# The inverses of an RWKV-7 chunk recurrence kept in 32 columns through four levels, with products over all four matrices' columns laid at steps of 96

## The chip, the cores and the metric

One core of one Trainium2 chip. The metric is the device time of one execution in microseconds. The kernel computes three layers (an RWKV-7 time mix, a differential attention, a gated linear recurrence with a spatial gate), each with its feed-forward part, on 256 tokens of width 1024, all in fp32.

## The reference, cut to what matters

The change lies in the RWKV-7 time mix: sixteen heads of 64 channels, 256 tokens, one token after another:

```
def step(state, inp):
    r_t, w_t, k_t, v_t, a_t, b_t = inp
    sa = jnp.einsum('bhvk,bhk->bhv', state, a_t)
    state = (state * w_t[:, :, None, :]
             + sa[..., None] * b_t[:, :, None, :]
             + v_t[..., None] * k_t[:, :, None, :])
    y_t = jnp.einsum('bhvk,bhk->bhv', state, r_t)
    return state, y_t
```

The kernel does it in chunks of 128 tokens. Within a chunk, `sa` of a token depends on `sa` of all earlier tokens through a strictly triangular 128x128 matrix A (products of `a` of one token and `b` of another, with the decay between them), so it needs the inverse of I - A, one for each head and chunk.

## The kernel before, in words

**Engines and order.** Each engine has its own program, written out by hand, and runs it strictly in order. Engines meet by semaphores. The eight PSUM banks are handed out ahead of time: `place(key, banks)` lists the jobs of each bank in their order; TensorE waits until the last use of the bank is freed (`open_bank`) and signals when its products are in (`close`); the reader waits for that (`wait_full`) and frees the bank (`release`). There are no costs or due times: what stands next on an engine is next.

**The recurrence.** It works on four pairs of groups (`PAIRS`, p = 0 to 3). A group `g` is 128 channels, so two heads; with two chunks of 128 tokens it has four matrices A, numbered j. For each pair:

1. Scores (L865 to L868): four products for each matrix, of 64 rows, into one bank. VectorE multiplies the bank with a mask of triangles (L2022) and so puts `scores` in SBUF. TensorE then does a stage of another kind, `project_r(p + 1)`, the projection for the next pair (three products at a time, L638 to L640); in pair 3 it does `y_centre` (L817) instead, whose results ScalarE writes in seven pieces of work (`y_square`, L1370 and L1371, and a table load).
2. The inverse of I - A, by doubling. `x` holds the inverse of the diagonal blocks of 2^l tokens, `xt` its transpose. A level l joins two neighbouring blocks: `y` is the product of A, as it lies in `scores`, with `xt` (L889), copied by ScalarE to SBUF (L1410), then `dx` = `y` with `x` (L901), of which VectorE takes the blocks of this level with a predicated copy (`joined`, L2029) and transposes 32x32 blocks (`turned`, L2025) to have `xt` for the next level. Up to block size 32 that transpose is all within 32x32 blocks (levels 0 to 4, below `SQUARE = 5`). At level 5 the blocks are 64 wide, so TensorE transposes (L912) and ScalarE copies (L1415). At level 6 only the corner of 64x64 is wanted: `y` (L891), the copy, `dxt` (L903), and VectorE's copy L2053.
3. The states and outputs: `q0`, `sa0`, `st`, `q1`, `sa1`, `yt` (L941 to L965), each one after another, with ScalarE's copies (L1441) and VectorE's L2079.

`x`, `xt` and `y` of one group are each 128x512: four matrices of 128 columns side by side, in `work[:, g % 2, i, :]`. Outside the diagonal blocks they are zero. Each level does group 0 of the pair, then group 1: eight `y` products, then eight `dx` products (four each).

**Side work.** Between the levels of pair p stands what prepares pair p + 1: on VectorE `decay_scan` (L1920) after level 1, `key_floor` (L1937) and `decay_centre` after 2, `decay_ends` after 3, `keys_unit` after 4, `keys_scaled` and `bonus_terms` after 5, the four `tilde` products after 6; on ScalarE the split of a weight unit (L1211) after 1, `key_log` (L1340) after 2, which waits for `key_floor`, `key_root` (L1344) after 3, `decay_now` after 4, `decay_sums` (L1358, L1360) after 5; on TensorE `key_sum` (L782) after 1.

Of the kernel before, what the change touches and what calls it, by code (L numbers as in the profile page):

```python
# [8 lines left out]
I32 = mybir.dt.int32  # L9
# [13 lines left out]
SQUARE = 5  # L23
NG = KT
# [48 lines left out]
CONS = [("ident", P), ("ones", P), ("head_sum", P), ("right_left", LEV * P), ("left_right", LEV * P), ("score_mask", 4 * P), ("centre", P), ("rope_swap", P), ("cos", S), ("sin", S)]  # L73
# [76 lines left out]
def build(nc, wide, down, x_t, ctx_t, cols, cons, rows, w_sp, out):  # L150
    with ExitStack() as ctx:
# [125 lines left out]
        for p, pair in enumerate(PAIRS):  # L277
# [12 lines left out]
            for l in range(1, LEV):  # L290
                for what in ("y", "dx") if l < SQUARE else ("y", "dx", "xt") if l < LEV - 1 else ("y", "dxt"):
                    for g in pair:
                        place((what, g, l), CHAIN_BANKS)
# [203 lines left out]
        y_sq = buf[1]  # L497

# [84 lines left out]
        with nc.Block() as block:  # L583
# [31 lines left out]
            def _(pe):  # L615
# [238 lines left out]
                for p, pair in enumerate(PAIRS):  # L854
                    nxt = p + 1 < len(PAIRS)
                    pe.wait_ge(sem("tilde_ready"), 4 * p + 4)
                    for g in pair:
                        for c in range(2):
                            for hd in range(2):
# [5 lines left out]
                                mm(bank[:, 0:P], at_, bt_, start=True, stop=True)  # L865
# [12 lines left out]
                    for l in range(1, LEV):  # L878
                        for g in pair:
                            xt = work[:, g % 2, 2, :]  # L880
                            if l <= SQUARE:
                                pe.wait_ge(sem(f"xt_ready{g % 2}"), SQUARE * (g // 2) + l)
                            else:
                                wait_freed(pe, ("xt", g, l - 1))
                            bank = open_bank(("y", g, l))
                            for j in range(4):
                                s_ = slice(j * P, (j + 1) * P)
                                if l < LEV - 1:
                                    last = mm(bank[:, s_], scores[g % 2][:, j, 0:P], xt[:, s_], start=True, stop=True)  # L889
# [3 lines left out]
                        for g in pair:  # L893
                            _, x, xt, y = (work[:, g % 2, i, :] for i in range(4))
                            wait_freed(pe, ("y", g, l))
                            what = "dx" if l < LEV - 1 else "dxt"
                            bank = open_bank((what, g, l))
                            for j in range(4):
                                s_ = slice(j * P, (j + 1) * P)
                                if what == "dx":  # L900
                                    last = mm(bank[:, s_], y[:, s_], x[:, s_], start=True, stop=True)  # L901
                                else:
                                    last = mm(bank[0:CH, j * CH:(j + 1) * CH], x[0:CH, j * P:j * P + CH], y[0:CH, j * CH:(j + 1) * CH], start=True, stop=True)  # L903
                            close(last, (what, g, l))
                        if SQUARE <= l < LEV - 1:
                            for g in pair:
                                x = work[:, g % 2, 1, :]
                                wait_freed(pe, ("dx", g, l))
                                bank = open_bank(("xt", g, l))
                                for j in range(4):  # L910
                                    s_ = slice(j * P, (j + 1) * P)
                                    last = nc.tensor.transpose(bank[:, s_], x[:, s_], ident)  # L912
                                close(last, ("xt", g, l))
# [148 lines left out]
                def context_states(c):  # L1062
                    if c == 4:
                        pe.wait_ge(sem("ctx_log"), 1)
                        for d in range(2):
                            tri = const("score_mask", (0, 2)[d] * P)
# [118 lines left out]
            def _(eng):  # L1185
# [160 lines left out]
                def units(g):  # L1346

                    act_(work[:, g % 2, 1, :].rearrange("p (j n) -> p j n", j=4), spread(ident, [P, 4, P]), ACT.Copy).then_inc(sem("unit_x"), 1)
# [42 lines left out]
                for p, pair in enumerate(PAIRS):  # L1391
# [13 lines left out]
                    for l in range(1, LEV):  # L1405
                        for g in pair:
                            key = ("y", g, l)
                            wait_full(eng, key)
                            m, n = (P, 512) if l < LEV - 1 else (CH, 4 * CH)
                            release(act_(work[0:m, g % 2, 3, 0:n], bank_of(key)[0:m, 0:n], ACT.Copy), key)  # L1410
                        if SQUARE <= l < LEV - 1:
                            for g in pair:
                                key = ("xt", g, l)
                                wait_full(eng, key)
                                release(act_(work[:, g % 2, 2, :], bank_of(key)[:, :], ACT.Copy), key)  # L1415
# [1155 lines left out]
```

## Time and profile before

| | us |
|---|---|
| median of 3 runs | 1399.5 (1395.93 to 1400.88) |
| the profiled execution's own time | 1391.34 |
| its span | 1389.3 |
| recurrence within the span, from the first scores (L865) to the last `yt` (L965) | about 99.5 to 324 |

Busy over the span: TensorE 1253.1 us (90%), VectorE 937.6 (67%), ScalarE 634.1 (46%), GpSimd 206.5 (15%). The chain of work that ended last is 64% TensorE, 24% VectorE, 7% ScalarE. An fp32 product has two records on TensorE. Records of one line that follow each other are merged, so `x8` beside L889 is four products; the time of such a row holds the tail of its last product. The granted clock is given as a share of full speed (2.4 GHz); 0.50 is 1.2 GHz.

### The profile page before, as it was taken

The page shows a single profiled execution, that of the slowest core. Times are in us where ns is not written, and L with a number is a line of the kernel's source. Part 1 is how long each engine was busy: PE and PEld are TensorE (multiplying, and loading weights), DVE is VectorE, ACT ScalarE, POOL GpSimd, SP SyncE. Part 2 cuts the span into 40 slices and gives each one's busy share as a digit, 9 for nine tenths or more (in the row PEclk, how much of TensorE's full clock was granted, in tenths as well). Part 3 has the DMA queues.
Part 4 walks back from the last instruction along what each step waited for, and adds up shares of the span by engine and source line. Part 5 has one row for each costly group of instructions (what it writes and reads, how often), then busy time and mean ns, then how long its engine had stood idle before and what let it go on. Part 6 is the DMA issues. An engine that isn't in the chain of part 4 may idle for free.

```text
span 1389.3 us, 21888 instructions
## 1 busy us (share of the span) xinstructions
PE 1253.1 (90%) x9218; PEld 1165.7 (84%) x9218; DVE 937.6 (67%) x1294; ACT 634.1 (46%) x835; POOL 206.5 (15%) x139
## 2 busy tenths in 40 slices
PE   4998988989899999699878889999789887999995
PEld 3887878777899999696658888999789877999995
DVE  6767566554478874646864666874558835999994
ACT  4464343253543445555555565434433234544442
POOL 0000000000454441000000111210000002344431
PEclk9999999899899999899998999999899998999998
DMA  7441001001676654253223677875333213555530
GB/s 270 146 162 33 32 1 62 1 1 48 244 250 247 243 183 152 93 186 115 98 89 119 212 267 269 292 276 183 109 138 113 74 57 121 183 170 184 185 130 31
DMA packets 122656, 200.26 MB, mean 144 GB/s; under 512 B 3264, under 2 KB 111168, under 8 KB 112320
## 3 DMA queue, kind: packets, MB, share of 16 engines
q1 hardware_dynamic: 117664, 168.11, 35.8%
q0 software_dynamic: 3456, 25.17, 4.8%
q10 hardware_dynamic: 1440, 5.60, 1.1%
q8 instruction: 73, 1.20, 0.3%
q14 instruction: 23, 0.19, 0.0%
HBM read 197.82 MB, written 1.05 MB: 143 GB/s over the span
## 4 chain that ended last, share of the span: by engine, by line
PE 64%; DVE 24%; ACT 7%; issue 4%; DMA 0%; DVEq 0%; POOL 0%; ACTq 0%
PE bank L638 13%; PE bank L639 12%; PE bank L640 12%; DVE buf L2453 7%; DVE ring_r L1760 6%; PE bank L721 3%; PE bank L723 3%; PE bank L722 3%; ACT high L1211 3%; PE bank L901 2%; DVE work L2029 2%; PE bank L654 2%; DVE work L2025 2%; PE bank L889 2%; PE bank L1103 1%
## 5 line engine op out<-in xcount | busy, mean ns | idle before, releaser
L638 PE MATMUL bank<-part,high 128*128 128x256 f32 x1664 | 486.8, 293 | 58.9 <-DVE part L1767 51.1
L1760 DVE TENSOR_TENSOR ring_r<-ring,high 128x2048 fp32r<-128x2048 f32 (+1 forms) x155 | 343.8, 2227 | 205.8 <-ACT high L1211 203.5
L639 PE MATMUL bank<-part,high 128*128 128x256 f32 x1664 | 481.7, 290 | 0.0
L640 PE MATMUL bank<-part,ring_r 128*128 128x256 f32 x1664 | 481.2, 289 | 0.0
L638 PEld LDWEIGHTS bank<-part,high 128*128 128x128 f32 x1664 | 330.9, 199 | 66.0 <-issue 41.9
L639 PEld LDWEIGHTS bank<-part,high 128*128 128x128 f32 x1664 | 331.0, 199 | 1.3 <-issue 1.2
L640 PEld LDWEIGHTS bank<-part,ring_r 128*128 128x128 f32 x1664 | 330.7, 199 | 0.0
L1211 ACT ACTIVATE high<-ring 128x2048 fp32r<-128x2048 f32 x155 | 295.1, 1906 | 51.1 <-PE bank L640 40.9
L1687 POOL TENSOR_TENSOR ring_r<-ring,high 128x512 fp32r<-128x512 f32 x44 | 92.7, 2107 | 523.4 <-ACT high L1211 523.3
L721 PE MATMUL bank<-part,high 128*128 128x256 f32 x528 | 151.3, 286 | 9.2 <-POOL part L1681 4.9
L722 PE MATMUL bank<-part,high 128*128 128x256 f32 x528 | 150.1, 284 | 0.0
L723 PE MATMUL bank<-part,ring_r 128*128 128x256 f32 x528 | 150.0, 284 | 0.0
L1681 POOL TENSOR_TENSOR part<-buf,part 128x256 fp32r<-128x256 f32 x66 | 100.0, 1517 | 224.6 <-ACT part L1266 224.6
L721 PEld LDWEIGHTS bank<-part,high 128*128 128x128 f32 x528 | 102.1, 193 | 10.2 <-POOL part L1681 5.2
L2453 DVE SCALAR_TENSOR_TENSOR buf<-buf,col 128x256 f32<-128x256 f32 x176 | 106.6, 606 | 5.5
L722 PEld LDWEIGHTS bank<-part,high 128*128 128x128 f32 x528 | 102.1, 193 | 0.3 <-issue 0.2
L723 PEld LDWEIGHTS bank<-part,ring_r 128*128 128x128 f32 x528 | 102.0, 193 | 0.0
L2109 DVE SCALAR_TENSOR_TENSOR buf<-buf,buf 128x1024 f32<-128x1024 f32 x64 | 100.2, 1565 | 1.4
L1266 ACT ACTIVATE part<-buf 128x256 fp32r<-128x256 f32 x66 | 27.5, 417 | 150.5 <-DVE buf L1821 150.5
L638 PE MATMUL bank<-high,part 128*128 128x512 f32 x144 | 60.1, 418 | 0.4 <-DVE buf L2172 0.4
L639 PE MATMUL bank<-ring_r,part 128*128 128x512 f32 x144 | 57.8, 401 | 0.0
L640 PE MATMUL bank<-high,part 128*128 128x512 f32 x144 | 57.6, 400 | 0.0
(267 smaller groups left out, 1568.5 us busy)
## 6 DMA issues: line engine op xcount, KB each, us to landing
ring<-in_wide SPq DMA_DIRECT2D x122, 1024.0 KB, 5.9
ring<-in_down SPq DMA_DIRECT2D x33, 1024.0 KB, 4.9
buf<-in_wide POOLq DMA_DIRECT2D x24, 1024.0 KB, 7.2
con<-in_cons SPq DMA_DIRECT2D x1, 1536.0 KB, 11.1
ring<-in_wide SPq DMA_DIRECT2D x2, 576.0 KB, 7.0
buf<-in_wide ACTq DMA_DIRECT2D x1, 1024.0 KB, 5.1
buf<-in_wide SPq DMA_DIRECT2D x1, 1024.0 KB, 5.2
buf<-in_ctx_t ACTq DMA_DIRECT2D x1, 1024.0 KB, 7.3
```

The lines of the kernel that those rows point to most:

```text
L638: mm(bank, ah, bh, start=start, stop=False, skip_group_check=shared)
L639: mm(bank, ah, bl, start=False, stop=False, skip_group_check=shared)
L640: return mm(bank, al, bh, start=False, stop=stop, skip_group_check=shared)
L721: mm(bank, wh, act_high(f), start=f == 0 and cb % 2 == 0, stop=False, skip_group_check=True)
L722: mm(bank, wh, act_low(f), start=False, stop=False, skip_group_check=True)
L723: return mm(bank, wl, act_high(f), start=False, stop=f == FT - 1, skip_group_check=True)
L1211: act_(hi, raw, ACT.Copy).then_inc(sem("unit_high"), 1)
L1681: nc.gpsimd.tensor_tensor(act_low(f), act_value(f), act_high(f).bitcast(F32), ALU.subtract).then_inc(sem("act_ready"), 1)
L1687: nc.gpsimd.tensor_tensor(low, raw, hi.bitcast(F32), ALU.subtract).then_inc(sem("unit_low_rest"), 1)
L1760: v.tensor_tensor(low, raw, hi.bitcast(F32), ALU.subtract).then_inc(sem("unit_low"), 1)
L2109: own.step(v.scalar_tensor_tensor(flat(buf[6])[:, 0:D], w, 1.0, silu_row[:, which, :], ALU.mult, ALU.mult, accum_out=ada[:, 4 * c + 2 * ha ...
L2453: ins = v.scalar_tensor_tensor(acc, view, pcol("conv_w", 9 * f + n), acc, ALU.mult, ALU.add)
```

## The change

- `x` is kept in 32 columns a matrix through levels 0 to 4 (`work[:, g % 2, 3, P:2P]`, 128 columns for the four matrices): row i holds the 32 columns of its own diagonal block of 32. `y` is kept likewise. `xt` stays at full width (512 columns).
- A product takes the 128x128 matrix of one j as the stationary side and the 128 columns of all four matrices as the moving side. Of the result only the 32 columns of matrix j are wanted; it is laid at column 96 j, so that these land at column 128 j, and the next product overwrites what isn't wanted.
- The stationary side of `y` is now A masked to its 32x32 diagonal blocks (`near`), and at level 5 A's blocks beside them (`far`), which ScalarE copies during level 1 (`far_blocks`).
- Level 0 goes into `xt` first and is transposed back to `x`. At levels 1 to 4 the join writes `x` (128 columns), and four transposes of 32 partitions each write `xt`. The product `y` waits for `x` alone, the product `dx` for `xt`.
- Level 5 has no transpose on TensorE: `corner` products and `dx` products give the two orientations. ScalarE copies `x`'s diagonal and the corner into `left_of(g)`, VectorE transposes two blocks a group into `xt`.
- The scores' matrix A is formed the other way round, and one more 64x64 product a matrix gives the corner in the first orientation. The constants grow by `later`, `near` and `joins`; four memsets are added at the start; the context sums read `later`.

The diff, cut to its core:

```
 for l in range(1, LEV):
-    for what in ("y", "dx") if l < SQUARE else ("y", "dx", "xt") if l < LEV - 1 else ("y", "dxt"):
+    for what in ("y", "dx") if l < SQUARE else ("y", "corner", "dx") if l < LEV - 1 else ("y", "dxt"):
...
 y_sq = buf[1]
+def chain_parts(g):
+    t = work[:, g % 2]
+    return t[:, 0, :], t[:, 1, :], t[:, 2, :], t[:, 3, 0:P], t[:, 3, P:2 * P]
+def left_of(g):
+    return work[0:CH, g % 2, 3, 2 * P:4 * P].rearrange("p (j n) -> p j n", j=4)
+def wide_y(g):
+    return work[0:CH, g % 2, 3, 0:4 * CH]
+def own_cols(j):
+    return slice(j * (P - SQ), j * (P - SQ) + P)
+def own_squares(t):
+    return t.rearrange("p (j n) -> p j n", j=4)[:, :, 0:SQ]
+def squares(t):
+    return t.rearrange("p (j n) -> p j n", j=4)
...
 at_, bt_, kt_, rt_ = (z[part, g, tok] for z in (kk_t, b_t, k_t, r_t))
-mm(bank[:, 0:P], at_, bt_, start=True, stop=True)
+mm(bank[:, 0:P], bt_, at_, start=True, stop=True)
+mm(bank[CH:P, 0:CH], at_[:, CH:P], bt_[:, 0:CH], start=True, stop=True)
...
 for g in pair:
-    xt = work[:, g % 2, 2, :]
+    near, far, xt, _, x = chain_parts(g)
     if l <= SQUARE:
-        pe.wait_ge(sem(f"xt_ready{g % 2}"), SQUARE * (g // 2) + l)
+        pe.wait_ge(sem(f"x_ready{g % 2}"), SQUARE * (g // 2) + l)
     else:
-        wait_freed(pe, ("xt", g, l - 1))
+        wait_freed(pe, ("dx", g, SQUARE))
+    if l == SQUARE:
+        pe.wait_ge(sem(f"far_ready{g % 2}"), g // 2 + 1)
         if l < LEV - 1:
-            last = mm(bank[:, s_], scores[g % 2][:, j, 0:P], xt[:, s_], start=True, stop=True)
+            last = mm(bank[:, own_cols(j)], (near if l < SQUARE else far)[:, s_], x, start=True, stop=True)
 for g in pair:
-    _, x, xt, y = (work[:, g % 2, i, :] for i in range(4))
+    _, _, xt, y, _ = chain_parts(g)
     wait_freed(pe, ("y", g, l))
+    if l <= SQUARE:
+        pe.wait_ge(sem(f"xt_ready{g % 2}"), SQUARE * (g // 2) + l)
+    else:
+        wait_freed(pe, ("corner", g, SQUARE))
+    if l == SQUARE:
+        bank = open_bank(("corner", g, l))
+        for j in range(4):
+            last = mm(bank[0:CH, own_cols(j)], xt[:, j * P:j * P + CH], y, start=True, stop=True)
+        close(last, ("corner", g, l))
     for j in range(4):
-        s_ = slice(j * P, (j + 1) * P)
-        if what == "dx":
-            last = mm(bank[:, s_], y[:, s_], x[:, s_], start=True, stop=True)
+        if l < SQUARE:
+            last = mm(bank[:, own_cols(j)], xt[:, j * P:(j + 1) * P], y, start=True, stop=True)
+        elif what == "dx":
+            last = mm(bank[0:P - SQ, own_cols(j)], xt[:, j * P + SQ:(j + 1) * P], y, start=True, stop=True)
         else:
-            last = mm(bank[0:CH, j * CH:(j + 1) * CH], x[0:CH, j * P:j * P + CH], y[0:CH, j * CH:(j + 1) * CH], start=True, stop=True)
+            last = mm(bank[0:CH, j * CH:(j + 1) * CH], left_of(g)[:, j, :], wide_y(g)[:, j * CH:(j + 1) * CH], start=True, stop=True)
     close(last, (what, g, l))
-if SQUARE <= l < LEV - 1:
-    for g in pair:
-        x = work[:, g % 2, 1, :]
-        wait_freed(pe, ("dx", g, l))
-        bank = open_bank(("xt", g, l))
-        for j in range(4):
-            s_ = slice(j * P, (j + 1) * P)
-            last = nc.tensor.transpose(bank[:, s_], x[:, s_], ident)
-        close(last, ("xt", g, l))
...
 def units(g):
-    act_(work[:, g % 2, 1, :].rearrange("p (j n) -> p j n", j=4), spread(ident, [P, 4, P]), ACT.Copy).then_inc(sem("unit_x"), 1)
+    act_(squares(chain_parts(g)[2]), spread(ident, [P, 4, P]), ACT.Copy).then_inc(sem("unit_x"), 1)
+def far_blocks(g):
+    eng.wait_ge(sem("scores_in"), g + 1)
+    far = squares(chain_parts(g)[1])
+    own.go(act_(far[0:SQ, :, SQ:CH], scores[g % 2][0:SQ, :, SQ:CH], ACT.Copy))
+    act_(far[CH:CH + SQ, :, CH + SQ:P], scores[g % 2][CH:CH + SQ, :, CH + SQ:P], ACT.Copy).then_inc(sem(f"far_ready{g % 2}"), 1)
+def left_diagonal(g):
+    eng.wait_ge(sem(f"x_ready{g % 2}"), SQUARE * (g // 2) + SQUARE)
+    x = squares(chain_parts(g)[4])
+    for b in range(2):
+        r = slice(b * SQ, (b + 1) * SQ)
+        own.go(act_(left_of(g)[r, :, r], x[r, :, :], ACT.Copy))
+def left_corner(g):
+    key = ("corner", g, SQUARE)
+    wait_full(eng, key)
+    release(act_(left_of(g)[SQ:CH, :, 0:SQ], own_squares(bank_of(key)[SQ:CH, :]), ACT.Copy), key)
...
     wait_full(eng, key)
-    m, n = (P, 512) if l < LEV - 1 else (CH, 4 * CH)
-    release(act_(work[0:m, g % 2, 3, 0:n], bank_of(key)[0:m, 0:n], ACT.Copy), key)
-if SQUARE <= l < LEV - 1:
+    if l < LEV - 1:
+        release(act_(squares(chain_parts(g)[3]), own_squares(bank_of(key)[:, :]), ACT.Copy), key)
+    else:
+        release(act_(wide_y(g), bank_of(key)[0:CH, 0:4 * CH], ACT.Copy), key)
+if l == 1:
     for g in pair:
-        key = ("xt", g, l)
-        wait_full(eng, key)
-        release(act_(work[:, g % 2, 2, :], bank_of(key)[:, :], ACT.Copy), key)
+        far_blocks(g)
+if l == SQUARE:
+    for g in pair:
+        left_diagonal(g)
+    own.settle()
+    for g in pair:
+        left_corner(g)
...
     own.go(v.memset(ap, value))
+for i in range(2):
+    own.go(v.memset(work[:, i, 1, :], 0.0))
+    own.go(v.memset(work[0:CH, i, 3, 2 * P:4 * P], 0.0))
...
         release(v.tensor_tensor(scores[g % 2][:, j, :], bank_of(key)[:, :], const("score_mask", 0, 512), ALU.mult), key)
-def turned(g):
-    v.transpose(work[:, g % 2, 2, :], work[:, g % 2, 1, :]).then_inc(sem(f"xt_ready{g % 2}"), 1)
-def joined(g, l, block):
-    return v.copy_predicated(work[:, g % 2, 1, :].rearrange("p (j n) -> p j n", j=4),
-                             spread(const("right_left", l * P), [P, 4, P]).bitcast(I32), block)
+def turned(g, back):
+    xt, x = squares(chain_parts(g)[2]), squares(chain_parts(g)[4])
+    for b in range(4):
+        r = slice(b * SQ, (b + 1) * SQ)
+        dst, src = (xt[r, :, r], x[r, :, :])[::-1 if back else 1]
+        ins = v.transpose(dst, src)
+        own.go(ins) if b < 3 else ins.then_inc(sem(f"{'x' if back else 'xt'}_ready{g % 2}"), 1)
 for g in pair:
+    near, _, xt, _, _ = chain_parts(g)
         wait_freed(eng, ("sc", g, j))
-    own.step(joined(g, 0, scores[g % 2][:, :, 0:P]))
-    turned(g)
+    eng.sem_inc(sem("scores_in"), 1)
+    v.copy_predicated(squares(xt), spread(const("left_right"), [P, 4, P]).bitcast(I32), scores[g % 2][:, :, 0:P])\
+        .then_inc(sem(f"xt_ready{g % 2}"), 1)
+    own.go(v.tensor_tensor(squares(near), scores[g % 2][:, :, 0:P], spread(const("near"), [P, 4, P]), ALU.mult))
+    eng.wait_ge(sem(f"xt_ready{g % 2}"), SQUARE * (g // 2) + 1)
+    own.settle()
+    turned(g, True)
     for g in pair:
-        if l < LEV - 1:
+        if l < SQUARE:
             wait_full(eng, key)
-            release(joined(g, l, bank_of(key)[:, :].rearrange("p (j n) -> p j n", j=4)), key)
-            if l < SQUARE:
-                wait_freed(eng, key)
-                turned(g)
+            x = squares(chain_parts(g)[4])
+            block = own_squares(bank_of(key)[:, :])
+            v.copy_predicated(x, spread(const("joins", (l - 1) * SQ, SQ), [P, 4, SQ]).bitcast(I32), block).then_inc(sem(f"x_ready{g % 2}"), 1)
+            eng.wait_ge(sem(f"x_ready{g % 2}"), SQUARE * (g // 2) + l + 1)
+            eng.sem_inc(free[jobs[key][0]], 1)
+            turned(g, False)
+        elif l == SQUARE:
+            key = ("dx", g, l)
+            wait_full(eng, key)
+            xt = squares(chain_parts(g)[2])
+            block = own_squares(bank_of(key)[:, :])
+            own.go(v.transpose(xt[0:SQ, :, SQ:CH], block[0:SQ]))
+            release(v.transpose(xt[CH:CH + SQ, :, CH + SQ:P], block[CH:CH + SQ]), key)
             wait_full(eng, key)
-            wait_freed(eng, ("xt", g, l - 1))
+            wait_freed(eng, ("dx", g, SQUARE))
...
 z["left_right"] = np.concatenate([m.T for m in lv], 1)
-z["score_mask"] = np.concatenate([i > j, i <= j, i < j, i <= j], 1)
+z["score_mask"] = np.concatenate([(i < j) | ((i >= CH) & (j < CH)), i <= j, i < j, i <= j], 1)
+z["later"] = i > j
+z["near"] = (i < j) & (i // SQ == j // SQ)
+z["joins"] = np.concatenate([np.take_along_axis(m, i // SQ * SQ + np.arange(SQ)[None, :], 1) for m in lv[1:SQUARE]], 1)
```

## Rows read from the trace of the kernel before

**Rows 1.** Chain of waits, pair 2, level 4: start, duration (us), engine, tile, line.
```profile
238.47 1.16 PE bank L889 x8
239.62 0.91 PE bank L901 x8
...
240.56 0.75 DVE work L2029
...
241.33 0.71 DVE work L2025
242.04 0.63 DVE work L2029
...
242.69 0.72 DVE work L2025
```

**Rows 2.** Chain of waits, pair 2, from level 2 to level 3.
```profile
232.59 0.59 DVE buf L1937
...
233.20 0.63 ACT buf L1340
...
234.37 1.17 PE bank L901 x8
```

**Rows 3.** Chain of waits, pair 2, levels 5 and 6.
```profile
243.46 1.16 PE bank L889 x8
244.61 1.86 PE bank L901 x16
...
248.57 0.53 ACT buf L1358
...
249.12 0.63 ACT buf L1360
...
250.07 1.14 PE bank L903 x16
```

**Rows 4.** Windows, levels of pairs 2 and 3: columns as the view's heading.
```profile
core 0: us, PE busy (x) PEld busy (x) DVE busy (x) ACT busy (x) POOL busy (x), PEclk, DMA share, GB/s
221.70:251.20 29.50, 25.05 (x205) 21.96 (x203) 19.69 (x35) 15.88 (x25) 0.00 (x0) 1.00 0.21 72
278.90:309.80 30.90, 26.59 (x208) 22.82 (x207) 14.18 (x21) 15.32 (x26) 0.00 (x0) 1.00 0.00 1
```

**Rows 5.** Groups by shape, 98 to 344 us: busy, mean ns; idle before.
```profile
L2029 DVE COPY_PREDICATED work<-con,bank 128x512 f32<-128x512 int32 x40 | 28.7, 718 | 40.4 <-PE bank L901 40.3
L2025 DVE STREAM_TRANSPOSE work<-work 128x512 f32<-128x512 f32 x40 | 28.5, 712 | 1.4
...
L1441 ACT ACTIVATE work<-bank 128x128 f32<-128x128 f32 x32 | 8.9, 278 | 23.3 <-PE bank L944 12.6 <-PE bank L951 10.6
...
L2079 DVE SCALAR_TENSOR_TENSOR work<-bank,tiny,con 128x128 f32<-128x128 f32 x8 | 2.8, 351 | 11.8 <-PE bank L955 11.8
```

**Rows 6.** Timeline of VectorE, pair 2: start, time of all, line, shape, count.
```profile
212.07 4.87 DVE L2022 TENSOR_TENSOR buf<-bank,con 128x512 f32<-128x512 f32 x8 [5.19 <-PE bank L868]
...
227.53 1.33 DVE L1920 TENSOR_TENSOR_SCAN buf<-con,buf 128x128 f32<-128x128 f32 x4
```

**Rows 7.** Timeline of ScalarE, pair 3, first copies of level 1.
```profile
281.77 1.08 ACT L1410 ACTIVATE work<-bank 128x512 f32<-128x512 f32 x2
```

**Rows 8.** Timeline of TensorE, in pair 2 and in pair 3.
```profile
225.44 1.02 PE L782 MATMUL bank<-buf,con 128*128 128x512 f32 x2
...
286.88 1.95 PE L889 MATMUL bank<-work,buf 128*128 128x128 f32 x16
```

**Rows 9.** Windows around and after the levels; PEclk is the granted clock.
```profile
196.00:208.00 12.00, 12.00 (x79) 10.62 (x77) 6.57 (x10) 3.86 (x11) 0.00 (x0) 0.72 0.01 1
248.00:252.00 4.00, 3.15 (x39) 2.80 (x39) 2.62 (x6) 2.42 (x6) 0.00 (x0) 0.98 0.01 4
250.00:266.00 16.00, 15.93 (x71) 10.90 (x72) 6.14 (x9) 2.55 (x9) 0.00 (x0) 0.68 0.00 1
308.00:324.00 16.00, 15.53 (x124) 12.11 (x124) 11.02 (x23) 5.50 (x16) 0.00 (x0) 1.00 0.00 1
```

More of the change, by code:

```diff
@@ L23 @@
 SQUARE = 5
+SQ = 32
 NG = KT
@@ L71 @@
         ("conv_b", FT), ("conv_w", 9 * FT), ("b_ada", 48)]
-CONS = [("ident", P), ("ones", P), ("head_sum", P), ("right_left", LEV * P), ("left_right", LEV * P), ("score_mask", 4 * P), ("centre", P), ("rope_swap", P), ("cos", S), ("sin", S)]
+CONS = [("ident", P), ("ones", P), ("head_sum", P), ("right_left", LEV * P), ("left_right", LEV * P), ("score_mask", 4 * P), ("centre", P), ("later", P), ("near", P), ("joins", (SQUARE - 1) * SQ), ("rope_swap", P), ("cos", S), ("sin", S)]
 ROWS = [("sgu_g", 512), ("sgu_b", 512), ("b_spatial", 512), ("lam", 256), ("c", 2 * D)]
@@ L1065, in context_states @@
                         for d in range(2):
-                            tri = const("score_mask", (0, 2)[d] * P)
+                            tri = const(("later", "score_mask")[d], (0, 2)[d] * P)
                             for t in range(TT):
```

## The prediction, as it was made

> **What bounds the kernel now.** I read the page first: TensorE is on 64% of the chain that ended last and VectorE on 24% (the table above). The change touches only the recurrence, so I then read the chain of waits there. In one middle level of a pair's inverses [rows 1] it is a closed loop: the second group's product L889, the first group's product L901, then four VectorE instructions in a row (join L2029 and transpose L2025, for the first group and the second). 243.46 (rows 3) - 238.47 = 5.0 us per level, of which VectorE has 2.8 us; TensorE's sixteen products need only 3.6 us (below). Level 3 is longer [rows 2]: key_floor L1937 stands on VectorE behind both groups, ScalarE's logarithm L1340 waits for it, and the copy of `y` (L1410) stands behind L1340; L901 waits for that copy. Levels 5 and 6 [rows 3] add transposes on TensorE (L912) with their copy L1415, and ScalarE's two exponentials L1358 and L1360 stand ahead of the level-6 copy, for which L903 waits. From the first product to the end of the last level it is 29.5 us for pair 2 (pairs 0 and 1 are alike within 0.1 us) and 30.9 us for pair 3 [rows 4]; TensorE is busy 85% of it, tails of waiting products included, so there is air of at least 4.4 us a pair.
>
> **Prices.** Back-to-back, sixteen records of 128-column products (two records a product, eight products) take 1.86 us with the tail [rows 3], so four products cost 0.9 us and a level's sixteen 3.6 us. Eight 64x64 products take 1.14 us [rows 3], with little tail 1.0. VectorE: a 128x512 join or transpose takes 718 or 712 ns, a 128x128 operation out of PSUM 351 ns [rows 5]. Back-to-back the cost is lower than the duration: eight 128x512 instructions in 4.87 us are 0.6 us each, four 128x128 scans in 1.33 us are 0.31 us each but for the tail [rows 6]. ScalarE: two copies of 128x512 take 1.08 us [rows 7], one of 128x128 278 ns [rows 5].
>
> **TensorE's work hardly changes.** The products of levels 1 to 4 keep 128 moving columns, four per group: same count, same price. Level 5 gets eight corner products (1.8 us) for eight transposes on TensorE, which are no dearer; the sum below counts the new ones in full. Scores get one 64x64 product for each of eight matrices of a pair: between 0.5 us (the two row halves overlap) and 1.0 us (1.14 us per eight, rows 3); I take 0.8 us. For pairs 0 to 2 it is on the path, because TensorE runs from scores through project_r without a gap into L889 at 221.70, where the stretch of rows 4 begins. For pair 3 it delays y_centre and so the seven ScalarE pieces that end at 281.77 [rows 7]: also 0.8 us.
>
> **VectorE, levels 1 to 4.** The join shrinks from 128x512 to 128x128: 0.35 us. The one transpose becomes four of 32x128 elements. The trace has no such row. Cheapest it is 0.2 us each (128 of the 512 elements of the 0.6 us rate, plus that rate's rest of 0.07 us), dearest 0.63 us (no cheaper than the whole one at its own rate, 712 ns less the 0.08 us overlap). I take 0.21 to 0.23, nearest to the scans and the 0.6 us row: 0.85 us for four, 1.2 us per group instead of 1.45. The larger gain is order: L889 now needs only the join (`x`), and the transposes `xt` are wanted only by the product after it, 1.8 us later. So per level, counted from the end of a group's second product: join to 0.35; TensorE is still in the other group's product until 0.9; transposes to 1.2; second group's join 1.2 to 1.55, wanted at 1.8. Nothing waits, ScalarE's copies (0.28) included: a level costs TensorE's 3.6 us.
> The Trainium skill, "VectorE: DVE Perf Modes", section on the TRN2 errata, says a fixed latency is paid per instruction, so many small tiles pay it each time, and gives about 150 cycles as the measured fixed part. By that (an estimate from the page) a transpose is 0.29 us, four are 1.16, and each level with side work on VectorE loses about another 0.5 us: some 4 us of the gain would go. The trace's 0.6 us rate [rows 6] says that back-to-back most of that term overlaps; the scans at 0.31 us stand nearer to the page.
>
> **The sum for a pair with a successor (0 to 2).** Level 1: 3.6 plus key_sum's one product of 512 columns, 1.02 us [rows 8] less its tail of some 0.16, so 4.45. Level 2: 3.6. Level 3: 3.6 plus the stall of rows 2, which stays: after the second product of level 2, VectorE has 2.4 us of joins and transposes and 0.65 us key_floor, ScalarE 0.65 us logarithm and 0.3 us copy, 4.0 us, where TensorE would want `y` at 2.7; so +1.35 (counted from the first group's product; until then TensorE has three groups' products of 0.9). Level 4: 3.6. Level 5: twenty-four products, 5.4. Level 6: two times 1.0 us, 0.2 us in which the second group's last two transposes are late, 0.3 us for the copy, 2.5 us. The exponentials L1358 and L1360 (1.16 us in the chain [rows 3]) start after left_corner, beside the second group's last products, and are done when the level-6 products are: they leave the path, and cost up to 1.2 us a pair if ScalarE is later than that. Loose ends 0.2. Total 24.7 against 29.5: 4.8, less 0.8 for scores, 4.0 us; three pairs 12.0 us.
> Pair 3 has no key_floor. Its levels 2 to 6 run from 286.88 [rows 8] to 309.8, 22.9 us; new 3 x 3.6 + 5.4 + 2.5 + 0.1 = 18.8. That saves 4.1, less 0.8: 3.3 us.
> Other edits cost nothing in their cover. The start of a pair: join L2029, the mask `near` and four transposes make 2.2 us per group instead of 1.4, so `x` of the second group is ready 4.4 us after the eighth score mask; VectorE finishes the masks at 216.9 [rows 6], so 221.4, ahead of 222.5 when L889 can start (221.70 plus 0.8). Uncovered it would be 1.6 us a pair; in pair 3, ScalarE's busy time to 281.77 covers it. far_blocks (four ScalarE copies, about 0.8 us per pair) fits in level 1; left_diagonal and left_corner lie beside the level-5 products. VectorE's keys_scaled and bonus_terms (five instructions, about 2.3 us) now end up to 1.3 us after L2053 is wanted; sa0 waits for L2053, but q0's products, about 1 us, come first, so 0.3 us, taken from the loose ends. Four memsets at the very start (under 2 us by the 0.6 us rate) lie beside the load of the input; uncovered they cost that once. The masks' load grows by 384 columns (196 KB on 1536) and is first needed far later.
> Together 15.3 us.
>
> **The clock.** After the level chains of pairs 0, 1 and 2 the granted clock falls to 0.50, the 1.2 GHz level, so that it is 0.72 over 12 us after pair 1 (pair 0 the same) and 0.68 over 16 us after pair 2, yet stays at 1.00 after pair 3 [rows 9]. In the 4 us before the third fall TensorE was busy 3.15 us. A mean of 0.72 over 12 us is 6.7 us at the low level, so at most 3.4 us lost; 0.68 over 16 us is 10.2, at most 5.1: together 11.9 us at stake. What pair 3 lacks before this place is just the wait behind L1358 and L1360, and that wait goes. The new levels also leave TensorE fewer pauses. But level 6 stays thin. The gain lies between 0 and 11.9 us; I take 5, a little under half, since parts of these stretches hang on ScalarE and VectorE.
> The Trainium skill, "TensorE: Matmul & The Clock Gate", on HAM oscillation, ties the fall to idle gaps between bursts; row 248:252 shows a fall with no such gap, so it gives no reason for the falls to go. By the page alone the clock term would be nothing.
>
> **Sum.** 15.3 + 5 = 20.3 us. The profiled execution took 1391.3 us (span 1389.3), so 1371.0. The median of three runs is 1399.5, 8 us above it; the saving carries over: 1379 us. What follows the recurrence starts earlier as a whole, as its first weights wait in the ring (SyncE's queue issues next to nothing in this stretch).
>
> **Rivals.**
> A. The clock stays full after all three pairs, and the waits shrink as counted: 15.3 + 11.9 = 27, 1372. For: pair 3. Against: thin level 6. Chance 0.18.
> B. Clock unchanged and VectorE as dear as the scans, so that levels 1 to 4 with side work are VectorE-bound: the scan rate makes 8 x 0.1 = 0.8 us more a level, of which side work exposes some 2 us a pair: 15.3 - 7 = 8 us, 1391. Chance 0.13.
> C. Slower: a small transpose costs as much as the whole one, 0.63 us. Then VectorE has 2 x (0.35 + 2.5) = 5.7 us per level plus side work (0.6 to 1.4 us in each of levels 1 to 4, as key_floor in rows 2 and the scans in rows 6), 27 us for four levels where it was 21.8 (221.70 to 243.46): with the scores +6 a pair, 1423 us. It decides from about 0.45 us per transpose on. Against: every other VectorE row shrinks with its elements [rows 5, 6]. Chance 0.05.
> D. The change doesn't shorten anything: as the products stay 128 columns wide, TensorE's busy time stays, and were TensorE the bound, only the added products would show: +3 us, 1402. Against: 15% air and rows 1. Chance 0.03.
> The forecast, 1379 (own range 1373 to 1387), has 0.61.
>
> Range 1367 to 1393: it takes in A and B, leaves C and D out. Under 0.3% (4.2 us) I could not tell from no change. Faster 0.92, same 0.03, slower 0.05.
>
> **What would show it.** Right: the level loop at 3.6 us with L889 following a join, not a transpose; a 32-partition transpose at 0.2 to 0.3 us; ScalarE's `y` copy at 0.28 us; a remaining TensorE wait of about 1.3 us before the second product of level 3; the stretches of rows 4 at 24 to 25 us; project_r 0.8 us later after the scores. Wrong: transposes of 0.4 us or more, chain steps at the transposes, scores that lose the overlap of their two row halves (over 1.5 us a pair), or new falls of the clock elsewhere.

## The result, and the profile after

The changed kernel takes 1411.8 us (median of 4 runs, 1410.9 to 1416.9) where the kernel before, beside it, takes 1400.2 (4 runs, 1395.9 to 1401.2): ratio 1.0097, 95% interval 1.0065 to 1.0128. It is slower by 11.6 us; forecast was 1379, faster by 20, in a range of 1367 to 1393. The sign is wrong.

The page of the profiled execution (1416.9 us, the highest of the four; the profiled execution of before was at 1391.3 among the lowest, so the two profiles differ by 25.8 us of span where the medians differ by 11.6; the mean granted clock of this execution is 0.942, of the other three 0.948 to 0.949):
```profile
PE 1282.1 (91%) x9314; PEld 1190.2 (84%) x9314; DVE 955.2 (67%) x1434; ACT 629.3 (44%) x867; POOL 206.4 (15%) x139
PE 65%; DVE 23%; ACT 6%; issue 5%; DMA 0%; DVEq 0%; POOL 0%; ACTq 0%
```

Windows of the profile after: the scores of pairs 0 to 3, then the levels of pairs 0 to 3 (start:end and length, then each engine's busy time and count, the granted clock, the DMA share and GB/s).
```profile
99.39:108.81 9.42, 9.42 (x82) 7.79 (x81) 6.49 (x8) 3.43 (x4) 0.00 (x0) 1.00 0.34 113
...
220.69:235.42 14.73, 14.73 (x81) 12.08 (x81) 4.84 (x7) 0.00 (x0) 0.00 (x0) 0.58 0.00 1
293.15:302.56 9.41, 9.41 (x82) 7.79 (x81) 4.84 (x7) 0.60 (x1) 0.00 (x0) 1.00 0.01 2
...
116.33:146.98 30.65, 27.29 (x213) 24.85 (x211) 20.59 (x60) 14.78 (x33) 0.00 (x0) 0.89 0.11 36
176.10:207.32 31.22, 27.62 (x213) 25.15 (x211) 20.94 (x63) 14.78 (x33) 0.00 (x0) 0.89 0.11 35
243.28:272.73 29.45, 26.20 (x213) 23.87 (x211) 20.00 (x59) 14.76 (x33) 0.00 (x0) 0.94 0.21 73
305.97:336.84 30.87, 27.82 (x215) 24.52 (x215) 16.26 (x51) 13.21 (x32) 0.00 (x0) 0.94 0.00 1
```
The levels were to shrink from 29.5 (pair 3: 30.9) [rows 4] to 24.7 (26.8) and have not shrunk: 122.2 us for the four pairs where before they took 119.4. By their granted clocks (each window times one minus its clock) at most 10.4 of the 122.2 us are the low clock's; before, the levels ran at full clock. The scores take 9.4 us a pair at full clock where before they took 5.0 (99.48 to 104.5 in the trace of before, for pair 0), and 14.7 us in pair 2, mostly at the low clock. With project_r behind pair 2's scores, 2.1 us slower for the same clock, the profiles' account is 22.9 (scores) + 2.1 + 2.8 (levels) = 27.8 us; the recurrence ends 27.0 us later (last L994 product at 350.74, before at 323.7). Everything is in the recurrence.

Two places explain it. **First the scores.** TensorE's timeline, one key (the products of one matrix) from 99.39 on:
```profile
99.39 0.48 PE L890 MATMUL bank<-buf,buf 64*128 64x128 f32 x2
99.81 0.33 PE L891 MATMUL bank<-buf,buf 64*64 64x64 f32 x2
100.06 0.49 PE L892 MATMUL bank<-buf,buf 64*128 64x128 f32 x2
...
100.61 0.38 PE L894 MATMUL bank<-buf,buf 64*128 64x128 f32 x2
100.92 0.33 PE L891 MATMUL bank<-buf,buf 64*64 64x64 f32 x2
```
From L891 to the next L891 it is 1.11 us. The same stretch of before:
```profile
100.25 0.27 PE L868 MATMUL bank<-buf,buf 64*128 64x128 f32 x1
100.36 0.27 PE L866 MATMUL bank<-buf,buf 64*128 64x128 f32 x1
100.37 0.27 PE L868 MATMUL bank<-buf,buf 64*128 64x128 f32 x1
100.47 0.27 PE L866 MATMUL bank<-buf,buf 64*128 64x128 f32 x1
```
There two products run at once, one in each 64-row half (records of L866 and L868 start 0.01 to 0.11 us apart), and a key, four products, comes every 0.55 us. After, L890 to L892 stand alone one behind the other; only the end of a key overlaps with the start of the next.

**Then VectorE in the levels.** Its timeline after, pair 1, levels 1 and 2:
```profile
179.19 0.30 DVE L2110 COPY_PREDICATED work<-con,bank 128x128 f32<-128x128 int32 x1 [2.08 <-PE bank L937]
179.64 1.31 DVE L2086 STREAM_TRANSPOSE work<-work 32x128 f32<-32x128 f32 x4
180.98 0.30 DVE L2110 COPY_PREDICATED work<-con,bank 128x128 f32<-128x128 int32 x1
181.43 1.30 DVE L2086 STREAM_TRANSPOSE work<-work 32x128 f32<-32x128 f32 x4
182.77 1.37 DVE L1976 TENSOR_TENSOR_SCAN buf<-con,buf 128x128 f32<-128x128 f32 x4
...
184.25 0.29 DVE L2110 COPY_PREDICATED work<-con,bank 128x128 f32<-128x128 int32 x1
```
A group is 1.79 us (179.19 to 180.98): join 0.30, 0.15 to the first transpose, then four transposes that start 0.33 us apart. Two groups are 3.58, as much as TensorE's whole level, and the scans with their copy (1.5 us) come on top: 5.06 us from level to level, no less than before [rows 1]. The groups by shape say the same; the y copy came out as costed:
```profile
L2086 DVE STREAM_TRANSPOSE work<-work 32x128 f32<-32x128 f32 x160 | 48.4, 303 | 10.0 <-DVE work L2110 1.0
...
L1457 ACT ACTIVATE work<-bank 128x128 f32<-128x128 f32 x40 | 10.7, 274 | 36.1 <-PE bank L917 35.7
```
The chain of waits after, pair 1, from level 2 to level 4 (start, duration, what):
```profile
186.03 0.31 DVE work L2110
186.39 0.44 issue
186.82 0.30 DVE work L2086
...
187.82 0.31 DVE work L2086
188.16 0.70 DVE buf L1993
188.89 0.63 ACT buf L1369
189.52 0.17 ACT work L1457
189.73 3.78 PE bank L937 x16
193.52 2.90 PE bank L917 x16
196.42 0.91 PE bank L937 x8
```
This is the place of [rows 2]: key_floor (L1993) behind the transposes, logarithm, y copy. TensorE's timeline shows what it costs there, in idle time and behind it:
```profile
189.73 3.78 PE L937 MATMUL bank<-work 128*128 128x128 f32 x16 [2.19 <-ACT work L1457]
193.31 3.11 PE L917 MATMUL bank<-work 128*128 128x128 f32 x16
196.25 1.95 PE L937 MATMUL bank<-work 128*128 128x128 f32 x16
```
Sixteen records are 1.95 us at full clock and 3.78 behind the 2.19 us wait. The windows give the granted clock:
```profile
186.00:190.00 4.00, 1.43 (x9) 1.24 (x10) 2.89 (x7) 1.10 (x4) 0.00 (x0) 0.86 0.03 6
190.00:194.00 4.00, 4.00 (x20) 4.00 (x21) 1.81 (x6) 1.78 (x2) 0.00 (x0) 0.50 0.00 0
...
222.00:238.00 16.00, 16.00 (x85) 13.54 (x82) 7.24 (x12) 0.00 (x0) 0.00 (x0) 0.53 0.00 1
```
After a 2.19 us pause the clock is at 0.50, the 1.2 GHz level; and it is at 0.53 over 16 us of pair 2's scores and project_r, in which TensorE never paused.

### The profile page after: what moved, and what is told of

Its sections match the earlier page's. It is cut to its first block, busy times and chain, and to the rows that moved or that the text cites. A ratio compares the mean times of both kernels' runs of the same rounds, so it can differ in the third digit from the quotient of the medians.

```text
span 1415.1 us, 22296 instructions
## 1 busy us (share of the span) xinstructions
PE 1282.1 (91%) x9314; PEld 1190.2 (84%) x9314; DVE 955.2 (67%) x1434; ACT 629.3 (44%) x867; POOL 206.4 (15%) x139
## 4 chain that ended last, share of the span: by engine, by line
PE 65%; DVE 23%; ACT 6%; issue 5%; DMA 0%; DVEq 0%; POOL 0%; ACTq 0%
PE bank L663 12%; PE bank L664 12%; PE bank L665 12%; DVE buf L2525 7%; DVE ring_r L1813 6%; PE bank L746 3%; PE bank L748 3%; PE bank L747 3%; ACT high L1240 3%; DVE work L2086 2%; PE bank L917 2%; PE bank L679 2%; PE bank L937 2%; PE bank L1132 1%; PE bank L892 1%
## 5 line engine op out<-in xcount | busy, mean ns | idle before, releaser
L1295 ACT ACTIVATE part<-buf 128x256 fp32r<-128x256 f32 x66 | 27.5, 417 | 150.6 <-DVE buf L1874 150.6
## 6 DMA issues: line engine op xcount, KB each, us to landing
con<-in_cons SPq DMA_DIRECT2D x1, 1728.0 KB, 11.6
```

## The experiments

Theory T: two terms were mis-sized. The odd-shaped score product ends the overlap of the two row halves (some 17 us), and the small transposes make VectorE the bound of the levels. Rivals: only one of them counts, or the clock alone. Each ratio is to the kernel before, run on the same chip beside it.

**1. The extra score product taken out of the change.** Level 6 is turned so that it needs no corner of the scores.
```diff
-mm(bank[CH:P, 0:CH], at_[:, CH:P], bt_[:, 0:CH], start=True, stop=True)
...
-last = mm(bank[0:CH, j * CH:(j + 1) * CH], scores[g % 2][CH:P, j, 0:CH], xt[CH:P, j * P + CH:(j + 1) * P], start=True, stop=True)
+last = mm(bank[CH:P, j * CH:(j + 1) * CH], scores[g % 2][0:CH, j, CH:P], left_of(g)[:, j, :], start=True, stop=True)
...
-last = mm(bank[0:CH, j * CH:(j + 1) * CH], left_of(g)[:, j, :], wide_y(g)[:, j * CH:(j + 1) * CH], start=True, stop=True)
+last = mm(bank[0:CH, j * CH:(j + 1) * CH], wide_y(g)[:, j * CH:(j + 1) * CH], xt[CH:P, j * P + CH:(j + 1) * P], start=True, stop=True)
```


> The changed kernel without the extra 64x64 score product: level 6 takes its block of A in the new orientation, with the inverse's left half (left_of) as the moving side, so the full result is still computed. Theory T (the extra product breaks the overlap of the two heads' row halves in the scores: 9.4 us a pair instead of 5.0): scores back to 5.0 us, 17 us less than the changed kernel, about 1394. Rival R (the score product costs only its columns, 0.8 us a pair, and the slowdown comes from the clock's falls and from the levels): 3 us less than the changed kernel, about 1408, and slower than before.

Measured: 1390.9 us (12 runs), ratio 0.9952 [0.9931, 0.9973]; against the changed kernel's 1.0097 that is 1.45%, 20 us. The scores are back at 5.0 us in every pair, the levels stay at 28.7 to 32.9. The score product alone costs more than the whole loss. Pair 0's levels rose to 32.9: with short scores the start of a pair is uncovered (below).

**2. The product put into the kernel before.**
```diff
+mm(bank[CH:P, 0:CH], at_[:, CH:P], bt_[:, 0:CH], start=True, stop=True)
 mm(bank[:, 0:P], at_, bt_, start=True, stop=True)
```


> The kernel before with one unused 64x64 score product a matrix put ahead of the first one, whose result is overwritten. T: scores at 9.4 us a pair, 17 us slower than before, about 1417. R: 0.5 to 1.0 us a pair, 1402 to 1404.

Measured: 1439.3 us (5 runs), ratio 1.0311 [1.0282, 1.0339]: +42 us, over twice what T gave. In the timeline of TensorE no two keys' products run at once any more, 1.34 us a key, so 10.7 us a pair at full clock:
```profile
169.25 0.33 PE L865 MATMUL bank<-buf,buf 64*64 64x64 f32 x2
169.50 0.48 PE L866 MATMUL bank<-buf,buf 64*128 64x128 f32 x2
...
170.27 0.38 PE L869 MATMUL bank<-buf,buf 64*128 64x128 f32 x2
170.59 0.33 PE L865 MATMUL bank<-buf,buf 64*64 64x64 f32 x2
```
The rest is the clock: in each pair's scores it falls, with TensorE busy throughout.
```profile
...
169.25:183.56 14.31, 14.31 (x82) 12.24 (x81) 4.84 (x7) 0.60 (x1) 0.00 (x0) 0.72 0.00 1
234.44:251.60 17.16, 17.16 (x81) 14.66 (x81) 4.84 (x7) 0.00 (x0) 0.00 (x0) 0.57 0.00 1
...
```
The scores of pairs 0 and 3 take 14.9 and 13.4 us (granted clock 0.69 and 0.78). Together the four are 59.7 us where before they were 20, so 39.7 of the 42 us. Place inside a key matters too: as the first product the odd one costs 5.7 us a pair, as the second (after) 4.4.

**3. The same product in the upper half of the output.**
```diff
+mm(bank[0:CH, 0:CH], at_[:, 0:CH], bt_[:, 0:CH], start=True, stop=True)
 mm(bank[:, 0:P], at_, bt_, start=True, stop=True)
```


> The kernel before with an unused 64x64 score product a matrix ahead of the first, as e2_before_corner, but laid in the upper half of the partitions. If the smaller shape of the product ends the overlap: 10.7 us of scores a pair, as e2. If it was its place in the lower half alone: about 6 us a pair, as e6.

Measured: 1438.3 us in one run, scores 13.4 to 17.8 us a pair, as in 2. Where the output lies is not it.

**4. The extra product with 128 stationary columns, as its neighbours.**
```diff
+mm(bank[:, 0:CH], at_, bt_[:, 0:CH], start=True, stop=True)
 mm(bank[:, 0:P], at_, bt_, start=True, stop=True)
```


> The kernel before with an unused extra score product a matrix as in e2_before_corner, at the same place, but with a stationary side of 64x128 as the other score products have (64 moving columns), where e2 had 64x64 laid in the lower half of the partitions. If it is the change of the tile's shape that ends the overlap of the two heads' products: overlap stays, scores 5.5 to 6.5 us a pair, 1399 to 1403. If any fifth product does it: 10 to 11 us a pair as in e2, 1435 or more.

Measured: 1397.9 us (10 runs), ratio 1.0004 [0.9983, 1.0025]; scores 6.8 us a pair:
```profile
99.33:106.14 6.81, 6.81 (x82) 6.69 (x81) 4.28 (x5) 3.43 (x4) 0.00 (x0) 1.00 0.48 157
```
More arithmetic, and 1.8 us a pair instead of 5.7: the cost is the change of the stationary operand's shape between 64x128 and 64x64, not the product.

**5. The corner products of two matrices together at the end**, so that the shape changes once per two keys.
```diff
-    mm(bank[CH:P, 0:CH], at_[:, CH:P], bt_[:, 0:CH], start=True, stop=True)
...
-    close(mm(bank[:, 3 * P:4 * P], kt_, rt_, start=True, stop=True), key)
+    mm(bank[:, 3 * P:4 * P], kt_, rt_, start=True, stop=True)
+for hd in range(2):
+    key = ("sc", g, 2 * c + hd)
+    part = slice(hd * CH, hd * CH + CH)
+    at_, bt_ = (z[part, g, c * P:(c + 1) * P] for z in (kk_t, b_t))
+    close(mm(bank_of(key)[CH:P, 0:CH], at_[:, CH:P], bt_[:, 0:CH], start=True, stop=True), key)
```


> The changed kernel with the two heads' 64x64 score products of a chunk put after the eight others of that chunk. T: the eight others overlap as before (1.2 us a chunk, 5.0 a pair), the two extra ones cost at most 0.25 us each: scores about 6 to 7 us a pair, 1400 to 1403. If the order has nothing to do with it (each change of tile shape costs the same wherever it stands): 9.4 us a pair, 1412 as the changed kernel.

Measured: 1404.9 us (7 runs), ratio 1.0047 [1.0015, 1.0079], 0.5% better than the change, though the intervals overlap; scores 7.7 us a pair, 1.8 us of the extra 4.4 gone. With half the changes of shape less is paid. But the two corner products that now stand together also run at once (four records of L898 in 0.33 us), so this run does not part the number of changes from the time of the odd products themselves.

**6. One transpose per join instead of four, score product kept.** The inverses of blocks 0 to 2 are left out.
```diff
-for b in range(4):
+for b in range(4) if back else (3,):
```


> The changed kernel with one of the four 32-partition transposes a join (blocks 0 to 2 are left out, so the inverses are wrong). If levels 1 to 4 are bound by VectorE (0.30 + 0.15 + 4 x 0.334 = 1.8 us a group, 3.6 us a level and side work on top), three transposes less take 2.0 us off VectorE's level: levels 1 to 4 shrink by 1 to 2 us each where there is side work, 12 to 20 us in all, about 1395. If they are bound by TensorE (3.6 us) and the stall at level 3, under 5 us, 1407 or more.

Measured: 1401.4 us (12 runs, 1385.8 to 1407.2; 1398.9 without the two at 1407, which the ratio leaves out too), ratio 1.0001 [0.9970, 1.0032], 13 us better than the change by the ratios. Pair 0's levels:
```profile
116.33:140.98 24.65, 23.76 (x213) 22.04 (x211) 13.33 (x36) 14.68 (x33) 0.00 (x0) 1.00 0.14 44
```
The other pairs: 24.9, 24.65 and 27.5. That is the predicted 24.7, so with cheap transposes the sum is reached in all; its terms are not all met, as the wait of TensorE before the second product of level 3 is 0.61 us here and not 1.35. By these windows 20.5 us left the levels of the four pairs, yet the two spans differ by 15.8. The scores of pair 2 stay at 14.9 us at the low clock, and behind pair 3's levels stands a fall that the change's execution does not have:
```profile
314.00:330.00 16.00, 16.00 (x49) 10.68 (x49) 7.36 (x16) 2.12 (x7) 0.00 (x0) 0.50 0.00 0
```

**7. The transposes made in another way** (in the change as it is): one 128x128 transpose straight from the product's bank, then one masked copy that lays the four blocks.
```diff
-eng.wait_ge(sem(f"x_ready{g % 2}"), SQUARE * (g // 2) + l + 1)
+own.step(v.transpose(turned_block(g), bank_of(key)[:, :].rearrange("p (j n) -> p j n", j=4)[:, :, 0:SQ]))
...
-turned(g, False)
+v.copy_predicated(wide(chain_parts(g)[2]), const("left_right", l * P)..., turned_block(g)...).then_inc(sem(f"xt_ready{g % 2}"), 1)
```


> The changed kernel, its extra score product kept, with the four small transposes of levels 1 to 4 replaced as in e7_one_turn. If the two faults are separate, it gains on the changed kernel what e7 gained on e4, 13 us: about 1399, levels of 26 us, scores still 9.4 us a pair. If the long scores already give VectorE its time back or the clock falls elsewhere, it gains less than 7 us, 1405 or more.

Measured: 1400.3 us (8 runs), ratio 1.0024 [1.0005, 1.0043], 10 us better than the change; levels 26.05 in pairs 0 to 2 and 27.9 in pair 3, at full clock. The ratio's interval lies wholly under the change's [1.0065, 1.0128].

**8. Both mended** (1 and 7).

> e4_level6_turned with the four 32-partition transposes of levels 1 to 4 replaced by one transpose of 128x128 out of PSUM into a spare tile (0.30 us) and one predicated copy of 128x512 from it into xt (0.6 to 0.7 us). Theory T (VectorE's 1.8 us a group, of which the four transposes are 4 x 0.334, sets the levels): a group costs 1.3 to 1.4 us, levels fall from about 30 us a pair to 26 to 28, 6 to 12 us less than e4, 1380 to 1385. Rival (the stall before the second product of level 3 and the fall of the clock behind it hold the levels, whatever the transposes cost): within 3 us of e4.

Measured: 1377.6 us (6 runs), ratio 0.9870 [0.9840, 0.9901]; levels 27.4, 26.0, 26.0 and 29.0. By ratios the score product is worth 1.45%, the transposes 0.73%, both together 2.27%: the two faults add, neither hides the other. The wait of TensorE before the second product of level 3 is 1.34 us in pairs 0 to 2, as predicted (1.35).

**9. key_floor one level earlier** (in 1), so that its logarithm no longer stands ahead of level 3's y copy.
```diff
 if l == 1:
     decay_scan(p + 1)
-elif l == 2:
     key_floor(p + 1)
+elif l == 2:
     decay_centre(p + 1)
```


> e4_level6_turned with key_floor taken from behind level 2 to behind level 1 on VectorE, so that ScalarE's logarithm no longer waits for the joins and transposes of level 2. If the 2.2 us in which TensorE waits at level 3 are that wait, and the clock falls because of it: no wait over 1 us there, no fall of the clock inside the levels of pairs 0 to 2, 2 us and up to 3 us of clock a pair, 1376 to 1384 in all. If VectorE's queue as a whole is the bound, the wait only moves to level 2 and the gain is under 3 us.

Measured: 1382.1 us (6 runs), ratio 0.9901 [0.9868, 0.9934], 7 us better than 1 by the ratios, with intervals that just overlap. Levels 30.6, 27.1, 27.1 and 29.1, in pairs 1 to 3 at a granted clock of 1.00 where 1 had 0.89, 1.00 and 0.94 (pair 0: 0.94, in 1 0.90). In pair 1 the fall went with the stall. That the stall brings it is likely, not shown: in pair 2 of run 1 the clock stays at 1.00 behind such a wait,
```profile
238.19 2.05 PE L936 MATMUL bank<-work 128*128 128x128 f32 x16 [1.84 <-ACT work L1456]
```
and pair 3, which has no key_floor, has a wait of 1.6 us in the change and in 1, 6, 7, 8, 9 and 11, with a fall behind it in the change, in 1 and in 8 and none in the other four. The transposes are as dear as they were.

**10. The same move in the kernel before.**

> The kernel before with key_floor taken from behind level 2 to behind level 1, as in e8_floor_early. If the gain of that move belongs to the new levels only (in the old ones the wait at level 3 is 0.56 us of TensorE): 1 us a pair, 3 us in all, 1394. If it is worth there what it brought on e4: 9 us less than before, 1388.

Measured: 1395.7 us (12 runs), ratio 1.0003 [0.9983, 1.0022]: levels 0.4 to 0.8 us shorter in pairs 0 to 2, nothing that shows in the time; the 3 us that were expected lie just outside the interval (at most 2.4 us). In this execution the granted clock is 0.50 over 306 to 326 us, behind pair 3's levels, where the kernel before has 1.00 in its trace.

**11. Everything mended:** 8 and 9, and ScalarE's key_square behind the first y copies instead of ahead of them.
```diff
 if nxt:
     side_out("r", p + 1, piece(r_t, p + 1))
-    key_square(p + 1)
...
 if l == 1:
+    if nxt:
+        key_square(p + 1)
     for g in pair:
         far_blocks(g)
```


> Both of the last two, and ScalarE's key_square behind the two y copies of level 1 instead of ahead of them. If their gains add: 1370 to 1378, with levels of pairs 0 to 2 at about 25 us, as the prediction had them. If one takes the place of the other: within 3 us of the better one.

Measured: 1374.6 us (6 runs), ratio 0.9832 [0.9797, 0.9868]: the fastest of all, 1.7% under the kernel before. Windows of its levels (the profiled execution is the fastest of the six, 1366.8 us):
```profile
112.56:138.38 25.82, 24.56 (x213) 22.37 (x211) 19.50 (x50) 15.02 (x33) 0.00 (x0) 1.00 0.13 42
160.58:184.71 24.13, 24.03 (x213) 22.23 (x211) 17.88 (x46) 15.02 (x33) 0.00 (x0) 1.00 0.13 45
...
257.99:285.59 27.60, 25.99 (x215) 23.16 (x215) 13.74 (x35) 13.01 (x31) 0.00 (x0) 1.00 0.00 1
```
In pairs 1 and 2 TensorE is busy 24.0 of 24.1 us: now it is the bound, at full clock. VectorE's group in its timeline:
```profile
168.11 0.29 DVE L2114 COPY_PREDICATED work<-con,bank 128x128 f32<-128x128 int32 x1
168.31 0.31 DVE L2115 STREAM_TRANSPOSE turn_tmp<-bank 128x128 f32<-128x128 f32 x1
168.76 0.75 DVE L2118 COPY_PREDICATED work<-con,turn_tmp 128x512 f32<-128x512 int32 x1
169.41 0.28 DVE L2114 COPY_PREDICATED work<-con,bank 128x128 f32<-128x128 int32 x1
```
1.30 us from group to group instead of 1.79. A 128x128 transpose takes 0.31 us, as long as a 32x128 one, and here it starts 0.20 us after the 0.29 us join: these two overlap, where the four small ones (each on 32 other partitions) do not. What keeps those apart no run tests.

## Why the prediction was wrong

**"Scores get one 64x64 product ... I take 0.8 us": the step that turned the sign.** I priced the product by its own rows [rows 3] and never asked what it does to its neighbours. It costs 4.4 us a pair at full clock (17.6 in all where 3.2 stood), because the products around it no longer run two at a time; 1, 2 and 4 show it from three sides, and 5 that fewer changes of shape cost less. In pair 2 the long scores also ran at the low clock, 5.3 us more. My own list of signs had it ("scores that lose the overlap ... over 1.5 us a pair"), but with no rival and no chance behind it. The trace of before showed what was at risk: pairs of L866 and L868 records a tenth of a microsecond apart. The Trainium skill, "TensorEngine Tiling (Array Packing)", Tiling Modes, Key Properties, says that changing the tiling mode, not just the tile, drains TensorE; it lists 64x128 and 64x64 as different configurations. Runs 2 and 4 agree with it (5.7 against 1.8 us a pair); I had not weighed it.

**"I take 0.21 to 0.23 ... 1.2 us per group": the step that took the gain.** Start to start it is 0.33 us, a group 1.79 us. I scaled down a 128x512 rate; the nearer row was the scans (0.31 us, rows 6), which are as short an instruction. The mechanism of rival B, VectorE as dear as the scans, came true, though I had priced it at 7 us: it is 30.65 - 24.65 = 6.0 us for pair 0 and 20.5 us in all four, since VectorE's four transposes delay the other group's join and key_floor as well; both figures hold the low clock, which stands behind the longer stall. 6 shows that with three of the four transposes out the levels come down to the sum. The rule of the Trainium skill that the prediction quoted ("VectorE: DVE Perf Modes", section on the TRN2 errata) made a transpose 0.29 us, an estimate from the page; measured are 303 ns, so the page was nearer than my choice.

**"Level 3 stall +1.35".** The stall stayed, longer (2.19 us idle), by the same cause: later transposes; with them mended (8) it is the 1.34 us of the sum. Not foreseen is the low clock behind it: in pair 1 the two stretches behind it take 6.7 us (3.78 + 2.90) where the same 32 records take some 3.6.

**The clock, +5.** Wrong in sign. In windows of 4 us over the recurrence the falls before (98 to 326 us) add up to at most 11.9 us lost (each window times one minus its granted clock); after (98 to 354 us), to 29 us: behind level 3's stall, behind the levels, and in the scores. Yet the idea under it, fewer pauses and a full clock, holds in the one execution of 11 that was profiled: it keeps 1.00 through all levels of all pairs, and in its recurrence one window of 4 us is low (186 to 190, 0.57).

**The start of a pair.** I wrote that masks and first transposes are covered until 222.5, if the scores take 0.8 us more. A group of them takes 2.8 us, not 2.2. With the scores 4.4 us longer they were covered, and with the scores short again (1) they were not, in pair 0 above all:
```profile
114.46 1.16 PE L916 MATMUL bank<-work 128*128 128x128 f32 x8 [0.83 <-DVE work L2085]
```
Level 1's first product began there at 112.58, waited 0.83 us for the second group's first transposes, and the second product began at 115.94, behind ScalarE's key_square (L1364 in that kernel) and the y copy: 1.6 us late, the 1.6 us that the prediction gave for the uncovered case. In pair 1 it was 0.4 us late (169.06 to 171.26, where 1.8 us are needed). 11 mends the ScalarE part: 1.1 us late in pair 0, not at all in pair 1.

**Right.** The first product of a level follows a join, the y copy is 0.27 us, level 5's and level 6's exponentials (L1405, L1407) left the path, TensorE's own work did not grow outside the scores, and the 24.7 of a pair's levels is what 6 measures (pair 3: 26.8 against 27.5), with some luck: 6 has less VectorE work than the sum (one transpose of four) and the shorter stall. The forecast of 1379 is 0.985 of the kernel before, within the intervals of 8 and 11, but by other terms: in 8 the levels gave 11.0 us where 18.5 were forecast, the scores cost nothing where 3.2 were, and the low clock took at most 3.4 us of the recurrence where before it took 11.9. Rivals A, C and D did not come about; a transpose is not as dear as the whole one (0.33 against 0.6).

**Open.** Why the clock falls where TensorE never pauses (scores of 9 to 17 us of 64-row products; behind the levels in the kernel before) isn't settled, nor why it does so in pair 2 and not in the others of the change, nor why waits of one length come with a fall and without one. The intervals of 8 and 11 overlap, so what key_floor and key_square add there (3 us by the medians) isn't shown by the time alone, only by the levels (26.0 to 24.1).

## What to carry to other kernels

Before a small product is put between others, look whether those run two at a time in the timeline; an extra product of the neighbours' shape may cost little where an odd shape costs the overlap. Work cut into a quarter of the elements is not a quarter of the time: for instructions of 128 elements per partition take the nearest short instruction's start-to-start time, and count what stands behind them on the engine. A loss can be two separate faults on top of a sound plan: mend one at a time, and look at the stages against the sum.

## What the runs showed of the hardware

- A 64x64 fp32 product among 64x128 ones costs 4.4 us per eight keys as the second product of a key, 5.7 as the first, 2.6 when two keys' stand together; with 128 stationary columns and 64 moving ones 1.8.
- A VectorE transpose of 128 fp32 elements per partition takes 303 ns on 32 partitions and 310 ns on 128; back-to-back in one group they start 334 ns apart, without overlap, where 128x512 operations overlap by some 0.07 us (eight of L2022 in 4.87 us [rows 6], so 0.61 each, against 0.68 for one).
- A masked copy whose source is repeated four times (128x512) takes 747 ns, about what a plain one takes (718) [rows 5].
- The granted clock went to 0.50 in stretches in which TensorE was busy all the time (2, 3, and pair 2 of the change), and the levels of 7 and 11 ran at 1.00.
